# Recurrence of a two-block decoder kernel: gates taken together, second head group begun later, one root for all heads

## What is computed

```python
def _hgrn2_mixer(h, w_in, lower_bound, out_norm, w_out):
    q, f, i, g = jnp.split(h @ w_in, 4, axis=-1)          # 8 heads of 128
    lb = lower_bound
    forget = lb + (1.0 - lb) * jax.nn.sigmoid(f)
    key_in = 1.0 - forget
    log_f = jnp.log(forget)
    o = _chunk_gated_recurrence(heads(jax.nn.silu(q)), heads(key_in), heads(i), heads(log_f))
    o = _rmsnorm_2(o, out_norm) * jax.nn.silu(heads(g))   # norm over each head's 128
    return o.reshape(B, S, D_MODEL) @ w_out
# S_t = diag(exp(log_f_t)) S_{t-1} + k_t v_t^T ; o_t = S_t^T q_t
# before it: x = rmsnorm(h, norm_final_w); h = rmsnorm(x, norm_mix)
```

## Time and profile before

| | |
|---|---|
| median of 3 runs | 1578.2 us (1575.36 to 1581.79) |
| profiled execution | 1581.98 us, span 1580.7 us |
| mean granted clock of PE | 0.956 |
| PE busy | 1422.9 us, 90% of the span |
| DVE busy | 867.4 us, 55% |
| ACT busy | 685.9 us, 43% |

### The profile page before, as it was taken

The page is one execution under the profiler, slowest core; times in us unless marked ns, Lnnn a source line. Parts: engine busy times, 40 slices in busy tenths (PEclk is TensorE's granted clock), DMA queues, the critical chain, the costliest instruction groups (busy, mean ns, idle before and its releaser), DMA issues. The chain is left out here.

```text
span 1580.7 us, 27550 instructions
## 1 busy us (share of the span) xinstructions
PE 1422.9 (90%) x11673; PEld 1205.9 (76%) x11673; DVE 867.4 (55%) x1544; ACT 685.9 (43%) x1188; POOL 10.6 (1%) x10
## 2 busy tenths in 40 slices
PE   7999999999999777777777777999999998899998
PEld 6999899899875434433433677989999986899997
DVE  6776463565512211111111557967888867678876
ACT  6443544544422111111110666555555566555553
POOL 1000000000000000000000100000000000000000
PEclk9999999999979998999998989989999998999999
DMA  7554354478889999999999543225555541446552
GB/s 234 160 161 147 120 161 134 160 261 287 352 349 424 425 425 422 426 426 424 425 426 426 186 134 106 82 82 176 172 202 192 170 121 53 134 160 201 193 175 99
DMA packets 173713, 372.05 MB, mean 235 GB/s; under 512 B 6912, under 2 KB 141184, under 8 KB 149008
## 3 DMA queue, kind: packets, MB, share of 16 engines
q1 hardware_dynamic: 173584, 370.22, 63.3%
HBM read 369.15 MB, written 1.05 MB: 234 GB/s over the span
## 5 line engine op out<-in xcount | busy, mean ns | idle before, releaser
L549 DVE TENSOR_TENSOR lo<-raw,hi 128x1024 fp32r<-128x1024 f32 (+2 forms) x315 | 377.1, 1220 | 202.2 <-ACT hi L538 201.2
L585 PE MATMUL bank<-XH,hi 128*128 128x256 f32 x1416 | 405.9, 287 | 8.2 <-DVE lo L549 5.7
L586 PE MATMUL bank<-XL,hi 128*128 128x256 f32 x1416 | 400.7, 283 | 0.0
L587 PE MATMUL bank<-XH,lo 128*128 128x256 f32 x1416 | 400.5, 283 | 0.0
L538 ACT ACTIVATE hi<-raw 128x1024 fp32r<-128x1024 f32 (+2 forms) x315 | 320.9, 1049 | 110.9 <-PE bank L587 40.6
L585 PEld LDWEIGHTS bank<-XH,hi 128*128 128x128 f32 x1416 | 271.5, 192 | 17.3 <-issue 10.8
L586 PEld LDWEIGHTS bank<-XL,hi 128*128 128x128 f32 x1416 | 271.4, 192 | 0.8
L587 PEld LDWEIGHTS bank<-XH,lo 128*128 128x128 f32 x1416 | 271.3, 192 | 0.0
L1707 PE MATMUL bank<-wu,xg 128*32 128x256 f32 x2048 | 170.2, 433 | 55.7 <-DMA wu<-in_expert_w_up_dram 49.8
L1707 PEld LDWEIGHTS bank<-wu,xg 128*32 128x32 f32 x2048 | 72.5, 120 | 128.2 <-DMA wu<-in_expert_w_up_dram 67.6
L1745 PE MATMUL bank<-wu,hidT 128*32 128x256 f32 x1024 | 73.2, 402 | 36.5 <-DMA wu<-in_expert_w_down_dram 27.0
(11 more groups left out here) (372 smaller groups left out, 2238.0 us busy)
## 6 DMA issues: line engine op xcount, KB each, us to landing
wu<-in_expert_w_gate_dram SPq DMA_DIRECT2D x64, 1024.0 KB, 26.6
wu<-in_expert_w_up_dram SPq DMA_DIRECT2D x64, 1024.0 KB, 26.3
wu<-in_expert_w_down_dram SPq DMA_DIRECT2D x64, 1024.0 KB, 26.8
raw<-in_w_in_dram SPq DMA_DIRECT2D x44, 1024.0 KB, 5.2
raw<-in_ffn_w_up_dram SPq DMA_DIRECT2D x44, 1024.0 KB, 5.1
raw<-in_ffn_w_down_dram SPq DMA_DIRECT2D x22, 1024.0 KB, 5.0
raw<-in_hgrn_w_in_dram SPq DMA_DIRECT2D x16, 1024.0 KB, 5.4
raw<-in_w_branch_ret_dram SPq DMA_DIRECT2D x8, 1024.0 KB, 7.0
```

What stands on the lines that cost most here:

```text
L549: dve.tensor_tensor(lo_of(u), v, hi_of(u), ALU.subtract).then_inc(*WL.inc(u))
L585: pe.matmul(dst, first[0], first[1], start=start, stop=False)
L586: pe.matmul(dst, second[0], second[1], start=False, stop=False)
L587: return pe.matmul(dst, third[0], third[1], start=False, stop=stop)
```

## The change

- `gained` moves to the memory of `o_`; it no longer lies over the buffers that `scaled` writes, and `scaled` no longer waits for the new `H`.
- `act_split(N1 + 6)` comes before the norm's root on ACT, and `dve_split(N1 + 4)` before `gained` and the sums on DVE. Of `act_first_out` only the root stays in its place (`act_first_root`); the two writes of `H` come after tile 5 is split.
- DVE scales tile 1 before it splits units 6 and 7.
- ACT gates tiles 4 to 7 together after tile 7. The exponentials of the first group come one step later on ACT (10 + 2L).
- The second group's levels come two steps later on PE (21 + 2L) and on DVE (19 + 2L); its k and all eight scans stand in one step (18) on DVE, its Ln at step 17 on ACT, and its exponentials at 20 + 2L.
- The sums of all eight heads go into one bank, followed by one root and one reciprocal. Silu of g is taken in four pieces, three of them in the third g tile. The gated products of heads 0 to 5 come before the reciprocal. All eight spreads are issued together, in banks 4, 6, 7 and 5. A table load for the root (`act_warm`) comes before the last side steps.

```diff
-    gained = at(gla_at, [P, 2, D], F32, "gained")
+    gained = at(m.place, [P, 2, D], F32, "gained")
...
+            act_split(N1 + 6)
             act.wait_ge(*S.dve.got("mean"))
...
-            dve_split(N1 + 3)
+            dve_split(N1 + 4)
             dve.wait_ge(*LD["wrow"].got())
...
-            dve_split(N1 + 4)
             dve.wait_ge(*S.act.got("g", 1, 1))
...
+        START = (8, 18)
         def pe_hgrn_heads(a):
-            yield from idle(8 + 8 * a)
+            yield from idle(START[a])
...
-            yield from pe_rstd(X, 4, tmps[a], 5 + 2 * a, 1)
...
+            for i in range(4):
+                h = h0 + i
+                pe.wait_ge(*X.act.got("sq", i))
+                pe.matmul(b_[5][0:8, 0:T], z[:, 7 - h:15 - h], tmps[a][:, i, :], start=(h == 0), stop=(h == 7)).then_inc(*X.pe.inc("sum", i))
+                if i % 2:
+                    yield
...
         def act_hgrn_heads(a):
-            yield from idle(4 + 8 * a)
+            yield from idle((4, 16)[a])
...
-            yield from idle(4)
+            yield from idle((5, 3)[a])
...
         def dve_hgrn_heads(a):
-            yield from idle(5 + 8 * a)
+            yield from idle((5, 17)[a])
...
-            yield
+            if a == 0:
+                yield
             for g in range(8):
...
-                if g % 4 == 3:
+                if a == 0 and g == 3:
                     yield
+            yield
...
+        def pe_hgrn_end():
+            pe.wait_ge(*HG.dve.got("rstd"))
+            for h in range(8):
+                X, b = HS[h // 4], bank[SPREAD[h // 2]]
+                for s, key in b.taken if h % 2 == 0 else []:
+                    pe.wait_ge(*s.got(*key))
+                pe_spread(X, b.ap[:, h % 2 * T:h % 2 * T + T], h, rowss[0][:, :])
+                b.taken = [(X.dve, ("scaled", h % 4))]
+
+        def act_hgrn_end():
+            act.wait_ge(*HS[1].pe.got("sum", 3))
+            act.activation(rowss[0][:, :], b_[5][0:8, 0:T], ACT.Sqrt, bias=epst[0:8, 0:1], scale=1.0 / 128).then_inc(*HG.act.inc("rms"))
+            act_hgrn_silu(3)
+            for h in range(8):
+                X = HS[h // 4]
+                act.wait_ge(*X.dve.got("scaled", h % 4))
+                act.activation(OH2[:, h, :], o_[:, h, :], ACT.Copy).then_inc(*X.act.inc("OH", h % 4))
...
+            for h in range(6):
+                gated(h)
+            dve.wait_ge(*HG.act.got("rms"))
+            dve.reciprocal(rowss[0][:, :], rowss[0][:, :]).then_inc(*HG.dve.inc("rstd"))
+            for h in range(9):
+                if h < 8:
+                    X = HS[h // 4]
+                    if h == 5:
+                        gated(6)
+                        gated(7)
+                    dve.wait_ge(*X.pe.got("spread", h | 1))
...
             for t, (name, j) in enumerate(kq_tiles):
                 act_tile(unit2(t), 2, AHEAD, sides)
-                gate(k_ if name == "k" else q_, ACT.Sigmoid if name == "k" else ACT.Silu, name, j)
+                if t == 5:
+                    act_first_out()
+
+                for n, i in {7: kq_tiles[4:]}.get(t, [(name, j)] if t < 4 else []):
+                    gate(k_ if n == "k" else q_, ACT.Sigmoid if n == "k" else ACT.Silu, n, i)
...
                 act_tile(unit2(12 + i), 2, AHEAD, sides, True)
-            for _ in range(12):
+                if i == 2:
+                    for j in range(3):
+                        act_hgrn_silu(j)
+            act_warm(ACT.Sqrt)
+            for _ in range(8):
                 step(*sides)
+            act_hgrn_end()
...
-                dve.wait_ge(*LAST.act.got("H", 1))
                 if t == 0:
...
-                dve_tile(unit2(t), 2, AHEAD, sides)
+                if t != 1:
+                    dve_tile(unit2(t), 2, AHEAD, sides)
...
                 scaled(t, k_ if name == "k" else q_, name, j)
+                if t == 1:
+                    dve_tile(unit2(t), 2, AHEAD, sides)
```

More of the change, by code:

```diff
@@ L458, in layout @@
     junk3 = at(m.place, [P, 8, 512], F32, "junk3")
-    gained = at(gla_at, [P, 2, D], F32, "gained")
-    v_, g_, S_, o_ = m.new([P, 2, D]), m.new([P, 8, T]), m.new([P, 8, 3, P]), m.new([P, 8, T])
+    v_, g_, S_ = m.new([P, 2, D]), m.new([P, 8, T]), m.new([P, 8, 3, P])
+    gained = at(m.place, [P, 2, D], F32, "gained")
+    o_ = m.new([P, 8, T])
     tmps, rowss = [m.new([P, 4, T]) for _ in range(2)], [m.new([8, T]) for _ in range(2)]
@@ L2094, in act_first_out @@
             act.activation(st[:, 36:38], st[:, 24:26], ACT.Sqrt, bias=epst[:, 0:1], scale=1.0 / D).then_inc(*S.act.inc("rootH"))
+        def act_first_out():
+            S = LAST
             act.wait_ge(*S.dve.got("rH"))
@@ L2153, in pe_hgrn_heads @@
             yield from pe_values(X, 4, S_[:, h0:h0 + 4, :, :], lambda h, blk, v: v_[:, blk, (h0 + h) * P:(h0 + h + 1) * P], 1, hgrn_pair(a))
-            yield from pe_rstd(X, 4, tmps[a], 5 + 2 * a, 1)
[L2155 to L2162, removed]
-            yield
+            z = C("zsel")
+            for s, key in bank[5].taken if a == 0 else []:
+                pe.wait_ge(*s.got(*key))
+            yield
+            for i in range(4):
[4 more added lines that the diff above has]
+                    yield
+            bank[5].taken = [(HG.act, ("rms",))]
         def act_hgrn_heads(a):
             X, h0, part = HS[a], 4 * a, slice(4 * a * T, (4 * a + 4) * T)
-            yield from idle(4 + 8 * a)
+            yield from idle((4, 16)[a])
             act.wait_ge(*LB.dve.got(5))
@@ L2172, in act_hgrn_heads @@
                                bias=lbt[:, 2, h:h + 1]).then_inc(*X.act.inc("ln", h - h0))
-            yield from idle(4)
+            yield from idle((5, 3)[a])
             yield from act_gated(X, 4, 1.0, c_[:, part], E_[:, part], S_[:, h0:h0 + 4, :, :], 4 + 2 * a, "K", 1)
             yield from act_values(X, 4, o_[:, h0:h0 + 4, :], hgrn_pair(a))
[L2176 to L2179, removed]
-            yield
[L2181 to L2184, removed]
+            for i in range(4):
+                act.wait_ge(*X.act.got("o", i - i % 2))
+                act.activation(tmps[a][:, i, :], o_[:, h0 + i, :], ACT.Square).then_inc(*X.act.inc("sq", i))
+                if i % 2:
+                    yield
         def dve_hgrn_heads(a):
             X, h0, part = HS[a], 4 * a, slice(4 * a * T, (4 * a + 4) * T)
-            yield from idle(5 + 8 * a)
+            yield from idle((5, 17)[a])
             dve.wait_ge(*LB.dve.got(5))
@@ L2202, in dve_hgrn_heads @@
                                  S_[:, h0:h0 + 4, :, :], hgrn_level(a), [(HG.act, ("q", 2 * a + 1))], "K", 1)
[L2203 to L2209, removed]
@@ L2210, in dve_hgrn_heads, with act_hgrn_silu @@
-            yield
-            for h in range(5):
-                if h < 4:
+        SPREAD = (4, 6, 7, 5)
+        def act_hgrn_silu(i):
+            act.wait_ge(*HG.dve.got("g", i))
+            act.activation(g_[:, 2 * i:2 * i + 2, :], g_[:, 2 * i:2 * i + 2, :], ACT.Silu).then_inc(*HG.act.inc("silu", i))
+        def pe_hgrn_end():
[3 more added lines that the diff above has]
+                for s, key in b.taken if h % 2 == 0 else []:
+                    pe.wait_ge(*s.got(*key))
+                pe_spread(X, b.ap[:, h % 2 * T:h % 2 * T + T], h, rowss[0][:, :])
+                b.taken = [(X.dve, ("scaled", h % 4))]
@@ new lines, in act_hgrn_end, with dve_hgrn_end, gated @@
+        def act_hgrn_end():
[6 more added lines that the diff above has]
+                act.activation(OH2[:, h, :], o_[:, h, :], ACT.Copy).then_inc(*X.act.inc("OH", h % 4))
+        def dve_hgrn_end():
+            def gated(h):
+                X = HS[h // 4]
+                dve.wait_ge(*HG.act.got("silu", h // 2))
+                dve.wait_ge(*X.act.got("sq", h % 4))
+                dve.scalar_tensor_tensor(o_[:, h, :], o_[:, h, :], PR("hgrn_norm", 0), g_[:, h, :], ALU.mult,
+                                         ALU.mult).then_inc(*X.dve.inc("gated", h % 4))
+            for h in range(6):
[4 more added lines that the diff above has]
+                if h < 8:
+                    X = HS[h // 4]
+                    if h == 5:
+                        gated(6)
+                        gated(7)
@@ L2213, in dve_hgrn_heads @@
                     dve.wait_ge(*X.pe.got("spread", h | 1))
-                    dve.wait_ge(*X.dve.got("gated", h))
-                    dve.tensor_tensor(o_[:, h0 + h, :], o_[:, h0 + h, :], b_[4 + 2 * a + h // 2][:, h % 2 * T:h % 2 * T + T],
-                                      ALU.mult).then_inc(*X.dve.inc("scaled", h))
+                    dve.wait_ge(*X.dve.got("gated", h % 4))
+                    dve.tensor_tensor(o_[:, h, :], o_[:, h, :], b_[SPREAD[h // 2]][:, h % 2 * T:h % 2 * T + T],
+                                      ALU.mult).then_inc(*X.dve.inc("scaled", h % 4))
@@ L2217, in dve_hgrn_heads @@
                 if h:
                     g = h - 1
[L2219 to L2221 removed]
+                    X = HS[g // 4]
```

(7 more changed lines are left out.)

5 lines of the change are left out of this document (3 added, 2 removed).

## The result

The changed kernel takes 1561.2 us (median of 5) against 1576.9 for the kernel before beside it: ratio 0.9897, 95% interval 0.9872 to 0.9922. Timed again it gave 0.9894 (0.9872 to 0.9916). Forecast were 1566 us and a gain of 12.4; about 15.5 came.

The account below looks back on a forecast made before the run. TensorE (PE), near nine tenths busy, was taken as the bound, so its waits and half-clock time counted. Removed waits and clock loss, less the new wait and tail loss, gave 12.4 us: 1578.2 to 1566, range 1558 to 1575.

Parts of the forecast that it names:

- rival A: Whole kernel: the gain comes as summed, 1566 us, own range 1562 to 1570; chance 0.5.
- rival B: Whole kernel: more is won than summed, 1560 to 1563 us; chance 0.2.
- B's two conditions: Late clock fall with spreads at full clock as far as OL allows (3.2 us), or the step 21 wait hidden (2.6).
- the wait at step 21: PE before score 5: a new wait of 2.6 us behind DVE's burst of k, eight scans and splits.
- Part 1 and 2: Recurrence start up to score level 0: earlier splits and reordered exponentials start score 0 5.4 us sooner.
- Part 3: Tiles 4 to 7, gates grouped: waits of 5.44, 0.81 and 2.43 us go, and 2.95 of half-clock loss.
- The sign "table loads for Sigmoid and Silu down by about six": ACT's table loads: about six fewer for Sigmoid and Silu would show the forecast right.
- The 5.44: PE's wait before score 2: 5.44 us, forecast to go, with 2.95 us lost to half clock behind it.
- too short for the clock: The 2.6 us wait before score 5 causes no half clock; falls came 3.9 and 4.6 us after work stopped.
- Part 4, the tail: Dense end to first OH matmul: 12.1 us against 8.67, loss 3.4; spreads start at 4.9, take 7.2 at half clock.
- Rival E: Steps 21 and 23: waits with clock falls make it slower, two about 1580 us, three 1588; chance 0.07.
- the 1.28 foretold: ACT's table loads before Q(4): 1.28 us each, without the skill's extra 1.38 drain.

Follow-up runs that it names:

- The front alone: Kernel before with only the splits ahead of the norm's sums, `gained` moved, `H` written after tile 5 and tile 1 scaled earlier: ratio 0.9985.
- the kernel with the gates old: Changed kernel with the gates of tiles 4 to 7 put back behind their own tiles: ratio 0.9937.
- the kernel with fillers before score 0: Changed kernel with 56 matmuls of 128x256 that nobody reads ahead of the wait of score level 0: 1565.1 us, ratio 0.9918.
- gates old, Ln early: Changed kernel with gates back behind their tiles, the second group's Ln back at step 13, its k and scans at 14 to 16: ratio 0.9929.
- gates and exponentials old: Changed kernel with gates of tiles 4 to 7 behind their tiles and the first group's exponentials one step earlier: ratio 0.9983.
- the tail with fillers: Changed kernel with 24 unread matmuls before the spreads and two after each pair of spreads: ratio 0.9912.

## Why the prediction was right, and where it was not

- **The number.** The measured 1561.2 lies just outside rival A's own range (1562 to 1570) and in rival B's (1560 to 1563). Of B's two conditions the first came in part: the clock fell late in the tail. The second did not: the wait at step 21 stayed.
- **Part 1 and 2** (5.4 us by score 0): measured 5.62. The front alone brought 3.39 (forecast by the same walk: 3.3); the exponentials one step later the remaining 2.3. The `lo` waits of 0.77 and 0.69 stand where 0.9 and a little were forecast. Shown by two experiments.
- **Part 3**: to score 4 the forecast gain was 17.0, the measured one 17.6 (93.77 to 76.15). The sum was right, its owner wrong. (The gain holds about 0.5 us of the clock: PE worked 4.3 us at half clock behind score 0, and 5.3 were charged.) "Gates of tiles 4 to 7 taken together" was named as what lets DVE keep up; put back, they cost 1.8 us by dense end. The sign "table loads for Sigmoid and Silu down by about six" came as three at the gates and three at the exponentials. The step had DVE's period right only because the walk contained the new order of the exponentials as well. By the landmarks that order is the larger edit, and the two overlap. The 5.44 itself came from three old orders together: the early second group with its Ln (5.40 to 1.84 without it), and the rest from gates and exponentials.
- **The new wait** before score 5: 2.6 forecast, 2.57 measured; no waits in the gating tiles, as taken. That it cost no half clock was forecast for a reason that does not hold in general: "too short for the clock", since falls had come 3.9 and 4.6 us after work stopped. Waits of 2.00, 2.28, 2.58 and 2.59 in four other kernels had a fall. The changed kernel passed it at full clock in both its profiles, but not because 2.6 us is always safe; so this term holds some luck.
- **Part 4, the tail**: the mechanism was right, a size was off. The spreads start at D+4.97 (4.9), but took 5.71 instead of 7.2: the clock fell 6.5 us after dense work, not before 4.9. Tail 10.6 instead of 12.1, so the loss is 1.9 rather than 3.4. This size is the clock's as well: in the eight profiles with this tail the fall came 5.1 to 7.2 us after dense end, and in the kernel with the gates old, where it came at 5.1, the first OH matmul stood 12.0 after dense end, as forecast. With 2.0 more won by the first OH matmul, 14.05 against 12.0, this is most of the difference; the rest of the recurrence gives 0.6.
- **Behind the recurrence** 1.4 us more went (first OH matmul to last matmul: 517.7 before, 516.4 after). No edit of any kernel here touches that part, and from the first H sum to the end the profiles differ by more than this: 514.2 us before, 512.8 and 512.8 in the changed kernel, 511.2 to 517.9 in the others. So the 1.4 is no part of the change that could be shown.
- Rival E needed two falls of the clock. None came in the changed kernel, but one line of order (Ln in front of two splits) was enough for 4.66 us and a fall, so its place was well named and its step too late by one score. That the changed kernel had none at its 2.57 is the luck named above.
- The Trainium skill, "ScalarE: Activation LUTs", What ACT_TABLE_LOAD costs, has a switch at 2.66 us. Here an ACTIVATE starts 1.30 us after its load, at 953.96 after 952.66; the wait at score 5 came as the 1.28 foretold.

## What to carry to other kernels

- When two engines hand work to each other in program order, compute the period of that loop and compare it with the engine that you feed. An instruction that waits should stand behind all work that waits for nothing: moving the exponentials behind the second split cost no instruction. By dense end it was worth 7.0 us, and the grouping with its six saved table loads (L2346 from 6 to 3, L849 from 5 to 2) 1.8; the times of the two kernels don't separate them.
- Two edits on one chain do not add: alone they gave 9.4 and 4.2 us by dense end, together 11.2. Name the owner of a gain only after undoing one.
- Count a deferred burst at its new place, and look who stands behind it: with the Ln ahead of two splits dense end came 4.0 us later than in the changed kernel, with the same Ln behind them 2.5 us sooner.

## What was not expected of the hardware

- The clock does not fall by the length of the wait alone. Waits of 2.57 and 2.58 us passed at full clock in the changed kernel; a wait of 2.59 at the same place brought a fall in the kernel with fillers before score 0, and so did one of 2.00 before score 4 in that with the gates back. Both falls came about 1 us after PE had resumed. Before score 3, waits of 2.58 (gates old, Ln early) and 2.28 (gates and exponentials old) had a fall 0.3 and 0.2 us before PE resumed.
- The time from the end of dense work to the fall in the tail was 4.0 us before, 6.5 after, and 5.1 to 7.2 over the eight profiles with the tail of the changed kernel.
- A busy PE is not enough to hold it: in the tail with fillers the clock fell within the spreads although PE had no idle time from dense end on. Which of the matmuls there (sums, fillers, spreads) let it fall is not shown.
- From the end of dense work to the first H sum one and the same tail program took 19.3 to 19.5 us in five profiles, with 10.2 us of half clock, and 17.7 to 17.9 in three, with 6.8. The two profiles of the changed kernel both belong to the five, so whether chance or the program decides is open. Either way 1.6 us of a difference between two profiles in this tail can be the clock's.
